# mLSTM's product with the old state: plain turned q, scaled by row behind the product and added in SBUF

## The reference: what is computed

```python
w_inter = jnp.exp(a - mt)                                  # one number per token and head
s = jnp.einsum('bhtd,bhsd->bhts', qb, kb) * jnp.exp(dmat - mt[..., None])
num = jnp.einsum('bhts,bhsv->bhtv', s, vb) + w_inter[..., None] * jnp.einsum('bhtd,bhdv->bhtv', qb, c)
den = jnp.sum(s, axis=-1) + w_inter * jnp.einsum('bhtd,bhd->bht', qb, n)
h = num / jnp.maximum(jnp.abs(den), jnp.exp(-mt))[..., None]
c_new = w_c[..., None, None] * c + jnp.einsum('bhs,bhsd,bhsv->bhdv', w_s, kb, vb)
```

## Time and profile before

| | before |
|---|---|
| median of the runs | 2675.71 us |
| the profiled execution: its span | 2674.2 us |
| TensorE (PE) busy | 2600.2 us, 97% of the span |
| VectorE (DVE) busy | 1879.2 us, 70% |
| ScalarE (ACT) busy | 905.2 us, 34% |
| GpSimd (POOL) busy | 77.1 us, 3% |
| a round of mLSTM | 29.35 us |

### The profile page before, as it was taken

The page is one execution under the profiler, slowest core; times in us unless marked ns, Lnnn a source line. Parts: engine busy times, 40 slices in busy tenths (PEclk is TensorE's granted clock), DMA queues, the critical chain, the costliest instruction groups (busy, mean ns, idle before and its releaser), DMA issues.

```text
span 2674.2 us, 41275 instructions
## 1 busy us (share of the span) xinstructions
PE 2600.2 (97%) x14365; PEld 2252.3 (84%) x14365; DVE 1879.2 (70%) x3249; ACT 905.2 (34%) x2072; POOL 77.1 (3%) x167
## 2 busy tenths in 40 slices
PE   7999999999999988999999899999899999999998
PEld 6888888877887868999999799999788888888887
DVE  6666676764544467777777888888877887885443
ACT  4333333443333343222222333233332332333332
POOL 0000000000000000000000000000000000000100
PEclk9999999999999999999999999999999999999999
DMA  5112111442322334212112432222242222234220
GB/s 205 56 56 82 55 55 68 160 147 95 109 107 89 106 113 164 86 63 63 63 63 66 158 123 63 93 83 74 72 143 78 78 74 72 74 139 143 71 88 36
DMA packets 164744, 249.56 MB, mean 93 GB/s; under 512 B 11120, under 2 KB 114648, under 8 KB 164664
## 3 DMA queue, kind: packets, MB, share of 16 engines
q1 hardware_dynamic: 162312, 239.97, 27.1%
q0 software_dynamic: 2352, 8.52, 1.0%
HBM read 191.34 MB, written 56.95 MB: 93 GB/s over the span
## 4 chain that ended last, share of the span: by engine, by line
PE 89%; DVE 7%; issue 1%; ACT 1%; DMA 1%; DVEq 0%; ACTq 0%; POOL 0%; SPq 0%; POOLq 0%
PE m_proj L112 12%; PE m_proj L114 12%; PE m_proj L113 12%; PE m_turned L112 6%; PE m_turned L114 6%; PE m_turned L113 6%; PE m_acc L114 5%; PE m_acc L112 5%; PE m_acc L113 5%; PE m_pair L112 4%; PE m_pair L113 4%; PE m_pair L114 4%; PE m_pair L1195 1%; DVE f_acc L2111 1%; PE m_turned L1203 1%
## 5 line engine op out<-in xcount | busy, mean ns | idle before, releaser
L1885 ACT ACTIVATE f_up_hi<-f_sums 128x512 fp32r<-128x512 f32 x144 | 89.5, 622 | 544.3 <-DVE f_sums L2067 496.9
L2083 DVE TENSOR_TENSOR f_part<-f_part,m_acc 128x384 f32<-128x384 f32 (+2 forms) x240 | 119.2, 513 | 144.5 <-PE m_acc L114 142.1
L112 PE MATMUL m_proj<-f_down_hi,f_uT_hi 128*128 128x512 f32 x512 | 204.5, 399 | 8.1 <-DVE f_acc L2111 7.8
L112 PE MATMUL m_turned<-f_down_hi,f_uT_hi 128*128 128x512 f32 x512 | 201.7, 394 | 10.2 <-DVE f_down_lo L2080 10.2
L113 PE MATMUL m_turned<-f_down_lo,f_uT_hi 128*128 128x512 f32 x512 | 201.2, 393 | 0.0
L114 PE MATMUL m_turned<-f_down_hi,f_uT_lo 128*128 128x512 f32 x512 | 201.0, 392 | 0.0
L114 PE MATMUL m_proj<-f_down_hi,f_uT_lo 128*128 128x512 f32 x512 | 200.8, 392 | 0.0
L113 PE MATMUL m_proj<-f_down_lo,f_uT_hi 128*128 128x512 f32 x512 | 200.5, 392 | 0.0
L2111 DVE TENSOR_TENSOR f_acc<-f_acc,m_turned 128x1024 f32<-128x1024 f32 x143 | 166.1, 1162 | 33.9 <-PE m_turned L114 31.7
L2111 DVE TENSOR_TENSOR f_acc<-f_acc,m_proj 128x1024 f32<-128x1024 f32 x128 | 155.8, 1217 | 46.7 <-PE m_proj L114 46.7
L1901 ACT ACTIVATE f_uT_hi<-f_part 128x256 fp32r<-128x256 f32 (+1 forms) x320 | 98.3, 364 | 206.7 <-PE m_turned L114 124.9
(11 more groups left out here) (374 smaller groups left out, 7174.4 us busy)
## 6 DMA issues: line engine op xcount, KB each, us to landing
f_up_raw<-in_w_up SPq DMA_DIRECT2D x96, 512.0 KB, 5.3
f_down_raw<-in_w_down SPq DMA_DIRECT2D x96, 512.0 KB, 5.2
hT_hi_kept<-m_hT_hi SPq DMA_DIRECT2D x17, 512.0 KB, 5.0
hT_lo_kept<-m_hT_lo SPq DMA_DIRECT2D x17, 512.0 KB, 5.8
a_hT_hi<-hT_hi_kept SPq DMA_DIRECT2D x17, 512.0 KB, 3.6
a_hT_lo<-hT_lo_kept SPq DMA_DIRECT2D x17, 512.0 KB, 4.5
m_x<-in_x_prompt SPq DMA_DIRECT2D x16, 512.0 KB, 4.3
a_x_sum<-in_x_prompt SPq DMA_DIRECT2D x16, 512.0 KB, 6.4
```

Of the source, the lines that this page charges most:

```text
L112: eng.matmul(out, lh(k), rh(k), start=f, stop=False)
L1885: act.activation(up_hi[:, q], weight(q), ACT.Copy).then_inc(up_hi_made, 1)
L2083: dve.tensor_tensor(part[out][:, 0:w], part[other][:, 0:w], up_ps[bank][:, 0:w], ALU.add).then_inc(combined, 1)
```

## The change

Before, q was scaled by row on VectorE, the scaled q was turned on TensorE and copied to SBUF by ScalarE, and its product with the old state went into the same PSUM sums as the weighted scores' product. Now the plain turned q, which is there for the scores anyway, is multiplied with the old state. This product stands ahead of the scores and goes into `m_turned` (four heads of 129 columns). VectorE scales it by row into a new SBUF tile `num`, and later adds the other product from `m_acc` to it. The denominator, the squares and the heads now read `num` instead of `m_acc`. The turning of the scaled q, its scaling and its copy are gone. `num` takes the place of the first weights buffer `w_raw`, and the squares' unused output is a tile of its own.

```diff
@@ -273,11 +273,13 @@
     x, gmix = sb("x", [P, 2, D]), sb("gmix", [P, D])
+    hT_hi, hT_lo = sb("hT_hi", [P, 2, KC, P], F32R), sb("hT_lo", [P, 2, KC, P], F32R)
+    num_at = sb.next
     w_raw = sb("w_raw", [P, PC])
-    hT_hi, hT_lo = sb("hT_hi", [P, 2, KC, P], F32R), sb("hT_lo", [P, 2, KC, P], F32R)
+    num = Place(nc, "m_", num_at, IDENT_AREA)("num", [P, HEADS, VA])
     q, k = sb("q", [P, 2, MW]), sb("k", [P, 2, MW])
     v, o = sb("v", [P, 2, HEADS, VA]), sb("o", [P, 2, MW])
-    qkT, qsT = sb("qkT", [P, 2, HEADS, P]), sb("qsT", [P, HEADS, P])
+    qkT, junk = sb("qkT", [P, 2, HEADS, P]), sb("junk", [P, HEADS, P])
     qT, kT = qkT[:, 0], qkT[:, 1]
@@ -333,14 +335,14 @@
     proj = [both[:, 0, :], both[:, 1, :]]
-    turned = ps("turned", [P, KC, P])
+    turned = ps("turned", [P, KC, P])[:]
     pair = ps("pair", [P, 2, NB])
...
     first_q, first_k = (acc[:, 2 * n:2 * n + 2, :].rearrange("p a b -> p (a b)") for n in (0, 1))
-    junk = qsT
+    past = turned.rearrange("p c t -> p (c t)").rearrange("p (h v) -> p h v", h=HEADS)[:, :, 0:VA]
@@ -522,10 +524,6 @@
                 act.activation(rows[:, LOG1P, 0:n], rows[:, F_EXP, 0:n], ACT.Ln, bias=1.0).then_inc(row_act, 1)
-            if exists(j):
-                all_of(act, qs_turned, j)
-                all_of(act, squared, j - 1)
-                act.activation(qsT[:, :, 0:mix.n], turned[:, 0:HEADS, 0:mix.n], ACT.Copy).then_inc(qsT_sb, 1)
             if on_round(r, NT):
@@ -543,15 +541,16 @@
             if exists(j):
-                all_of(act, num_ps, j)
+                all_of(act, num_sb, j)
                 reached(act, fin_step, (j - 1) * FIN_STEPS + 10)
                 for h in range(HEADS):
-                    ins = act.activation(junk[0:mix.n, h, :], acc[0:mix.n, h, 0:QK], ACT.Square, accum_out=fin[0:mix.n, 3, h:h + 1])
+                    ins = act.activation(junk[0:mix.n, h, :], num[0:mix.n, h, 0:QK], ACT.Square, accum_out=fin[0:mix.n, 3, h:h + 1])
                 ins.then_inc(squared, 1)
...
                 else:
+                    all_of(act, past_ps, j)
                     all_of(act, C_made, j)
@@ -562,7 +561,7 @@
             all_of(pe, normed, t.i, NORM)
-            all_of(pe, qsT_sb, t.i - 3)
+            all_of(pe, past_sb, t.i - 3)
             for c in range(KC):
@@ -628,7 +627,7 @@
                 else:
-                    all_of(pe, qsT_sb, j - 1)
+                    all_of(pe, past_sb, j - 1)
                 all_of(pe, q_sb, j)
@@ -644,19 +643,21 @@
             if exists(j):
-                all_of(pe, q_scaled, j)
                 all_of(pe, qT_sb, j)
                 all_of(pe, kT_sb, j)
+                if m == P:
+                    all_of(pe, C_moved, j - 1)
+                state = C if m == P else C_dec
                 for h in range(HEADS):
-                    ins = pe.transpose(turned[:, h, 0:m], q[0:m, mix.slot, h * QK:(h + 1) * QK], ident[0:m, 0:m])
-                ins.then_inc(qs_turned, 1)
+                    ins = pe.matmul(past[0:m, h, :], qT[:, h, 0:m], state[:, h, :], start=True, stop=True)
+                ins.then_inc(past_ps, 1)
                 all_of(pe, masked, j)
...
                 all_of(pe, v_sb, j)
-                all_of(pe, fin_step, j - 1, FIN_STEPS)
+                all_of(pe, num_sb, j - 1)
                 for h in range(HEADS):
@@ -671,15 +672,10 @@
             if exists(j):
-                all_of(pe, qsT_sb, j)
                 all_of(pe, weighted, j)
                 all_of(pe, C_made, j)
-                if m == P:
-                    all_of(pe, C_moved, j - 1)
-                state = C if m == P else C_dec
                 for h in range(HEADS):
-                    pe.matmul(acc[0:m, h, 0:VA], qsT[:, h, 0:m], state[:, h, :], start=True, stop=False)
-                    ins = pe.matmul(acc[0:m, h, 0:VA], decay[0:m, h, 0:m], v[0:m, mix.slot, h, :], start=False, stop=True)
+                    ins = pe.matmul(acc[0:m, h, 0:VA], decay[0:m, h, 0:m], v[0:m, mix.slot, h, :], start=True, stop=True)
                 ins.then_inc(num_ps, 1)
@@ -715,7 +711,7 @@
                 at = slice(h * QK, (h + 1) * QK)
-                ins = dve.scalar_tensor_tensor(heads_out[0:m, at], acc[0:m, h, 0:QK], fin[0:m, 7, h:h + 1], o[0:m, t.slot, at],
+                ins = dve.scalar_tensor_tensor(heads_out[0:m, at], num[0:m, h, 0:QK], fin[0:m, 7, h:h + 1], o[0:m, t.slot, at],
                                                ALU.mult, ALU.mult)
@@ -770,9 +766,6 @@
-                all_of(dve, cols_sb, j, 2)
-                qv = q[0:m, mix.slot, :].rearrange("p (h d) -> p h d", h=HEADS)
-                dve.tensor_tensor(qv, qv, cols[0:m, 4:8].unsqueeze(2).to_broadcast([m, HEADS, QK]), ALU.mult).then_inc(q_scaled, 1)
                 if on_round(r, NT + 1):
@@ -791,6 +784,10 @@
             if exists(j):
+                all_of(dve, past_ps, j)
+                all_of(dve, cols_sb, j, 2)
+                all_of(dve, fin_step, j - 1, FIN_STEPS)
+                dve.tensor_tensor(num[0:m], past[0:m], cols[0:m, 4:8].unsqueeze(2).to_broadcast([m, HEADS, VA]), ALU.mult).then_inc(past_sb, 1)
                 all_of(dve, scores_ps, j)
@@ -835,13 +832,15 @@
                 f = lambda a: fin[0:m, a, :]
-                all_of(dve, squared, j)
-                dve.tensor_tensor(f(0), acc[0:m, :, QK], cols[0:m, 8:12], ALU.max).then_inc(fin_step, 1)
+                dve.tensor_tensor(num[0:m], num[0:m], acc[0:m, :, 0:VA], ALU.add).then_inc(num_sb, 1)
+                all_of(dve, num_sb, j)
+                dve.tensor_tensor(f(0), num[0:m, :, QK], cols[0:m, 8:12], ALU.max).then_inc(fin_step, 1)
                 dve.wait_ge(fin_step, base + 4)
-                dve.scalar_tensor_tensor(f(1), acc[0:m, :, QK], -1.0, f(0), ALU.mult, ALU.max).then_inc(fin_step, 1)
+                dve.scalar_tensor_tensor(f(1), num[0:m, :, QK], -1.0, f(0), ALU.mult, ALU.max).then_inc(fin_step, 1)
                 dve.wait_ge(fin_step, base + 5)
...
                 dve.wait_ge(fin_step, base + 6)
+                all_of(dve, squared, j)
                 dve.tensor_tensor(f(4), f(3), f(2), ALU.mult).then_inc(fin_step, 1)
@@ -1236,7 +1235,7 @@
                 all_of(pe, kv_sb, 0)
-                pe.wait_ge(*m.qsT_sb)
+                pe.wait_ge(*m.past_sb)
                 turn_qk(cur)
```

More of the change, by code:

```diff
@@ L192 @@
     o_sb: object
-    qsT_sb: object
+    past_sb: object
     cols_sb: object
@@ L353, in mlstm_programs @@
     cols_ps, cols_sb, masked, decayed = (sem(n) for n in ("cols_ps", "cols_sb", "masked", "decayed"))
-    qk_turned, qT_sb, kT_sb, q_scaled, k_scaled = (sem(n) for n in ("qk_turned", "qT_sb", "kT_sb", "q_scaled", "k_scaled"))
-    qs_turned, qsT_sb, scores_ps, state_ps = (sem(n) for n in ("qs_turned", "qsT_sb", "scores_ps", "state_ps"))
+    qk_turned, qT_sb, kT_sb, k_scaled = (sem(n) for n in ("qk_turned", "qT_sb", "kT_sb", "k_scaled"))
+    past_ps, past_sb, num_sb, scores_ps, state_ps = (sem(n) for n in ("past_ps", "past_sb", "num_sb", "scores_ps", "state_ps"))
     weighted, C_made, C_moved, num_ps, squared, fin_step, out_done, state_out = (
@@ L856, in mlstm_programs @@
                     q_ps=(q_ps, NT + 1), k_ps=(k_ps, NT + 1), v_ps=(v_ps, NT + 1), o_ps=(o_ps, NT + 1), v_sb=(v_sb, NT + 1), o_sb=(o_sb, NT + 1),
-                    qsT_sb=(qsT_sb, NT + 1), cols_sb=(cols_sb, 2 * (NT + 1)), weighted=(weighted, NT + 1),
+                    past_sb=(past_sb, NT + 1), cols_sb=(cols_sb, 2 * (NT + 1)), weighted=(weighted, NT + 1),
                     heads_done=(fin_step, FIN_STEPS * (NT + 1)), out_done=(out_done, 16 * (NT + 1)), state_out=(state_out, 16 * 6), n_rows_sb=(n_rows_sb, 1))
```

## The result

The changed kernel takes 2734.2 us, the median of four runs (2733.29 to 2735.44); the kernel before takes 2675.9 us beside it (2674.64 to 2676.59). The ratio is 1.0218, with an interval of 1.0206 to 1.023. It is slower, as forecast, by 58.3 us instead of 39, and 2.2 us above the range.

The account below looks back on a forecast made before the run. The prediction took a loop through VectorE's half and ScalarE's gates to bound 14 rounds. 25.8 - 0.4 + 5.6 = 31.0 us, plus 8.5 for the clock, on 2674.2 gave 2713.7, median 2715; range 2700 to 2732.

Parts of the forecast that it names:

- the side, and the place: Slower by over 0.2%, chance 0.92, in 14 rounds bound by a loop through VectorE's second half and ScalarE's gates.
- TensorE's own work: In each round TensorE loses four turnings and has 0.44 us less to do; round 15 gains that.
- scores and increment later: Behind v, scores and state increment come 0.45 us later, and VectorE waits for both.
- the scaling free: VectorE's scaling of the product fits between v's copy and the scores, costing nothing beyond the 0.45 us.
- the add: VectorE's 128 x 516 add stands directly ahead of line 839 and lengthens each round by 0.73 us.
- the squares: ScalarE's squares, hidden before, now start after the add and take 1.14 us: +0.66 us a round.
- the sum: The added terms in one of the 14 rounds: 0.45 + 0.73 + 0.66 = 1.84 us, 25.8 us over 14.
- The upper bound of 1.6 us: Most that four squares from SBUF might take, from attention's exponentials at 0.40 us each: +0.45 more.
- the kernel before's stall: Ahead of line 616, TensorE waits some 0.25 us a round for ScalarE's copy of gates and o.
- the clock: The stall ahead of line 616 becomes 2.37 us; TensorE's clock falls in five of 14 rounds, 8.5 us.
- every round falls: Rival: TensorE's clock falls in every round, costing 24 us, 2731 us in all; chance 0.14.
- The start of attention: ScalarE, blocked in its queue until the last add, delays attention's first exponentials by 5.6 us.

Follow-up runs that it names:

- the gate buffer: The kernel before the change, with the finished gate in a buffer of its own and ScalarE's wait for the heads relaxed: 2674.21 us, ratio 0.9996.
- the kernel with 100 columns: The kernel before the change plus one useless VectorE reciprocal of 100 columns (0.76 us) ahead of each tile's finish: 2687.07 us, ratio 1.0043.
- the filler: The changed kernel plus sixteen unread turnings of a constant on TensorE in the wait ahead of line 615: 2709.91 us, ratio 1.0127.
- the add-early kernel: The changed kernel with VectorE's add moved ahead of the normalisation of the next x: 2703.28 us, ratio 1.0095.
- the 220-column delay: The kernel before the change plus one useless VectorE reciprocal of 220 columns (1.51 us) ahead of each tile's finish: 2700.71 us, ratio 1.0092.
- The runs with 340 columns: The kernel before the change plus one useless VectorE reciprocal of 340 columns (2.26 us) ahead of each tile's finish: 2727.55 us, ratio 1.0182.

## Why the prediction was right and where it was wrong

**Right: the side, and the place.** The 14 rounds are bound by the loop through VectorE's finish and ScalarE's gates. With that one wait relaxed, the same change gains 6.9 us in the rounds instead of losing 51.7.

**Right: TensorE's own work.** 0.44 us less per round were forecast, 0.43 measured (28.85 against 29.28). Round 15 gained 0.4 us as forecast.

**Right: scores and increment later, the scaling free.** The weighting starts 1.78 us behind the start of v's copy (402.26 - 400.48) against 1.33 before: +0.45, as forecast. The add starts where the finish's first step did, +0.46 (11.31 us behind the copy against 10.85). The scaling was free with nothing to spare: it ended at 402.24, and the 0.27 us of cover that the prediction saw were used up.

**Right: the add.** 412.49 - 411.79 = 0.70 us, forecast 0.73.

**Too small: the squares.** From the first step of the finish to the one that needs the squares it is now 413.98 - 412.49 = 1.49 us against 0.59: +0.90, where the sum had 0.66. Two parts make the difference: the four squares take 1.29 us (412.59 to 413.88) instead of 1.14, and ScalarE starts 0.13 us behind the add's end instead of the 0.05 of the sum, for which no row was given. The Trainium skill (VectorE: DVE Perf Modes, section on the TRN2 errata) would have made four squares 0.17 us dearer from SBUF; the trace has 0.15 and so agrees. The upper bound of 1.6 us, taken from exponentials with a bias tensor, was far off. The terms measured are 0.46 + 0.70 + 0.90 = 2.06, and heads and gates behind them 0.04 less; the base round grew by 2.08, where the sum had 1.84, so 0.06 lie outside this piece. Over 14 rounds this is 29.1 us against 25.8.

**Not quite right, without a cost: the kernel before's stall.** "TensorE stands still for some 0.25 us a round": the gate buffer shows 0.07.

**Wrong: the clock.** The step that failed is this: "Behind 2.18 it stayed at 1.00. 2.37 lies between. I take five falls in 14 rounds, 8.5 us; bounds 0 and 14 falls, 0 and 24 us." It was ten low rounds, and five of them lost 3 us, not 1.7: 22.6 us. Two things were wrong in it. Waits of later stages were taken as a scale for this loop: 2.18 us, behind which the clock held, as a bound below which it holds, and 2.51 us as one above which it falls. The runs show neither in the loop. Low rounds came behind stalls of 1.3 to 1.7 us too, two to five in 14; and the stall, forecast as 2.37, was 2.51 us or more in ten rounds, by that scale a fall in each of them, while three of these (5, 8 and 12) stayed at full clock. Nor was the wait of 2.18 us an accident of one profile: its clock held in all eleven, while behind the wait of 2.51 or 2.52 us in the MLP it fell in ten and held in one, the kernel with 100 columns:

```profile
1934.55 0.47 PE L112 MATMUL m_proj<-f_down_hi,f_uT_hi 128*128 128x512 f32 x1 [2.52 <-DVE f_acc L2113]
```

```profile
1934.50:1936.00 1.50, 1.45 (x7) 1.24 (x8) 1.50 (x3) 1.09 (x3) 0.00 (x0) 1.00 0.00 0
1936.00:1938.00 2.00, 1.51 (x7) 0.94 (x5) 2.00 (x4) 0.80 (x2) 0.00 (x0) 1.00 0.00 0
```

So in these traces the length of a wait alone doesn't say whether the clock falls behind it. And the loss per fall was taken from the two later waits alone. The experiments with the stall bridged (23.1 us back) and with the stall alone added (9 low rounds, 19 us) show that the low rounds come of the stall; nothing else in the change is needed for them. The time came nearest to the rival "every round falls", 2731 us; but its mechanism isn't what happened either, since four rounds were at full clock and the others lost up to twice its price.

The Trainium skill (TensorE: Matmul & The Clock Gate, section on HAM oscillation) tells of a kernel that paid the change of clock in every turn of its loop. The trace agrees in kind and not in number: ten of 14 turns here, two of 14 behind the shortest stalls that had any.

**Right: the start of attention.** Forecast +5.6 us, measured +5.8. From the start of round 16 the last add was to end at 44.8 us and ended at 44.9, and from there squares, copies and splits were to take 7.7 us and took 7.6 (590.05 to 597.67). What the prediction couldn't separate, the experiments did: 3.2 us come of the squares behind the late add, and 2.6 are VectorE's own added work. Of the 3.2 only 1.5 are ScalarE's queue alone; VectorE's operand was 4.3 us later than before, where the prediction had 2.4 and a wait for squares of less than that, so the block mattered less than it says.

The sum, against the span: 29.1 (loop) + 22.6 (clock) - 0.4 (round 15) + 5.8 (attention) = 57.2 of 58.3 us, before rounding. The 1.1 us left lie behind the first exponentials, and their cause stays open; with the filler the same remainder was -0.8, so it may be no more than the spread of single executions. Open stays, too, why the same stall of 2.52 us is followed by no fall, a short or a long one, and why the add-early kernel with 1.5 us had five low rounds and the 220-column delay with 1.4 only two. The runs with 340 columns, which differ by 11 us, say that something varies from execution to execution; one profile of each kernel can't tell how much. But within a profile the order isn't random. In the changed kernel each of the full-clock rounds 5, 8 and 12 is followed by a short fall, and from round 3 on each short fall by a long one; with 220 columns twelve rounds in a row, nearly alike in length and stall, stay at 1.00. When the stall comes, and not only how long it is, may thus matter; no run tests it.

## What to carry to other kernels

Before a step is put into a loop that two engines close, look for the wait that closes it, not for the busy shares: here VectorE was busy for 69% of a round and each microsecond added to its half still lengthened the round. Then price the stall that TensorE gets in each turn twice, once as time and once as clock: here stalls of 0.6 to 0.9 us cost themselves alone, those of 1.3 to 1.7 us another 0.2 to 0.9 us each on average (3.1 / 14 to 12.8 / 14), those of 2.5 us another 1.6 (22.6 / 14). And ask what resource the closing wait guards: one more buffer of 128 x 512 took away a loss of 52 us that came from far more visible operations.

## What the hardware showed that was not expected

- The granted clock fell behind stalls of 1.31 to 1.72 us in three kernels (10 of 42), though behind a wait of 2.18 us in a later stage it held in all eleven profiles. Behind 0.56 to 0.86 us it fell in none of 28.
- A fall in these rounds is of two kinds: 3 to 4 us at 1.2 GHz, beginning up to some 2 us after TensorE has started again (216.97, clock down from 219), or 6 to 7 us, when the clock is down just before it starts (250 to 257) or within 0.5 us behind it (started 175.58, down from 176). Where it is down before, the first matmul takes 0.76 us instead of 0.46.
- Sixteen 128 x 128 turnings of a constant, 1.91 us of work without use in a wait, kept the clock at 1.00 in all 14 rounds and gave back 23 us.
- ScalarE's square of 128 x 128 with a sum comes every 0.30 us from SBUF (1.29 for four), against 1.14 us for four from PSUM.
